# A fused attention, recurrence and MLP step: decode rows second in the output projection, and an up projection that begins before the last token tile is normalised

## What is computed

```
def merge_and_mlp(x, o_a, o_b, mg, w_br_a, w_br_b, w_out, ln1_g, ln1_b, w_up, w_down, ln2_g, ln2_b):
    br_a = jnp.einsum('bse,ed->bsd', o_a, w_br_a)
    br_b = jnp.einsum('bse,ed->bsd', o_b, w_br_b)
    merged = jax.nn.sigmoid(mg[..., :D_MODEL]) * br_a + jax.nn.sigmoid(mg[..., D_MODEL:]) * br_b
    mix = jnp.einsum('bsd,de->bse', merged, w_out)
    x1 = layer_norm(DEEPNORM_ALPHA * x + mix, ln1_g, ln1_b)
    h = jnp.einsum('bsf,fd->bsd', jnp.square(jax.nn.relu(jnp.einsum('bsd,df->bsf', x1, w_up))), w_down)
    return layer_norm(DEEPNORM_ALPHA * x1 + h, ln2_g, ln2_b)
```

## Time and profile before

| | us |
|---|---|
| median of three runs | 2279.09 |
| the three runs | 2273.63, 2279.09, 2280.14 |
| the profiled execution, its own time | 2276.24 |
| its span | 2274.4 |
| PE busy in the span | 2127.7 |
| DVE busy | 1084.1 |
| ACT busy | 744.9 |

### The profile page before, as it was taken

The page is one execution under the profiler, slowest core; times in us unless marked ns, Lnnn a source line. Parts: engine busy times, 40 slices in busy tenths (PEclk is TensorE's granted clock), DMA queues, the critical chain, the costliest instruction groups (busy, mean ns, idle before and its releaser), DMA issues.

```text
span 2274.4 us, 33288 instructions
## 1 busy us (share of the span) xinstructions
PE 2127.7 (94%) x13962; PEld 1804.7 (79%) x13962; DVE 1084.1 (48%) x2075; ACT 744.9 (33%) x1375; POOL 144.4 (6%) x157
## 2 busy tenths in 40 slices
PE   7999899979878999999999999979999999999994
PEld 6997677759548999998888874469888988898883
DVE  2037887746522566765211115544444444444447
ACT  3125666634321355544111112222112221122117
POOL 0021000001110122311000000000000000000003
PEclk9998999989999999999999999979999999999997
DMA  9222000046652232222212131111111111111001
GB/s 235 78 71 106 11 11 1 11 169 213 196 186 66 47 67 53 59 52 85 84 28 56 29 106 61 32 62 47 47 38 56 47 47 37 56 47 47 19 19 75
DMA packets 140193, 156.77 MB, mean 69 GB/s; under 512 B 25794, under 2 KB 122139, under 8 KB 135308
## 3 DMA queue, kind: packets, MB, share of 16 engines
q1 hardware_dynamic: 132012, 111.87, 16.2%
q0 software_dynamic: 8032, 42.78, 6.1%
HBM read 139.05 MB, written 19.76 MB: 70 GB/s over the span
## 4 chain that ended last, share of the span: by engine, by line
PE 85%; DVE 6%; DMA 4%; ACT 3%; issue 2%; SPq 0%; POOLq 0%; POOL 0%; DVEq 0%; ACTq 0%
PE PS L751 57%; PE PS L1294 5%; PE PS L1320 5%; PE PS L951 3%; PE PS L1018 2%; PE PS L932 2%; DMA arena<-in_cache_sel_kv,arena 2%; DVE arena L1794 1%; PE PS L904 1%; PE PS L1003 1%; DVE arena L1810 1%; PE PS L906 1%; DMA arena<-in_x_prompt 1%; PE PS L1220 1%; PE PS L1351 1%
## 5 line engine op out<-in xcount | busy, mean ns | idle before, releaser
L751 PE MATMUL PS<-x_low,w_high_mlp 128*128 128x344 f32 x1104 | 354.1, 321 | 0.0
L751 PE MATMUL PS<-w_down_high,hidden 128*128 128x512 f32 x1024 | 329.5, 397 | 9.9 <-DVE arena L2280 5.6
L751 PE MATMUL PS<-x_high,w_high_mlp 128*128 128x344 f32 x768 | 246.2, 321 | 5.2 <-DVE w_low L772 5.2
L751 PEld LDWEIGHTS PS<-w_down_high,hidden 128*128 128x128 f32 x1024 | 193.3, 189 | 67.9 <-DVE arena L2280 20.2
L751 PE MATMUL PS<-x_high,w_low 128*128 128x344 f32 x768 | 246.7, 321 | 0.0
L2280 DVE TENSOR_TENSOR arena<-arena,PS 128x512 f32<-128x512 f32 x256 | 175.2, 687 | 143.1 <-PE PS L751 143.1
L751 PEld LDWEIGHTS PS<-x_low,w_high_mlp 128*128 128x128 f32 x1104 | 208.1, 188 | 2.6
L751 PE MATMUL PS<-w_down_low,hidden 128*128 128x512 f32 x512 | 201.8, 394 | 0.0
L751 PE MATMUL PS<-x_low,w_high_hgrn 128*128 128x344 f32 x624 | 201.0, 322 | 0.0
L751 PE MATMUL PS<-x_high_a,w_low 128*128 128x344 f32 x480 | 154.7, 322 | 0.0
L751 PE MATMUL PS<-x_high_b,w_low 128*128 128x344 f32 x480 | 153.4, 320 | 0.0
(11 more groups left out here) (347 smaller groups left out, 4025.2 us busy)
## 6 DMA issues: line engine op xcount, KB each, us to landing
wring<-in_w_in SPq DMA_DIRECT2D x100, 256.0 KB, 3.4
wring<-in_w_up SPq DMA_DIRECT2D x64, 256.0 KB, 3.3
arena<-in_w_down SPq DMA_DIRECT2D x16, 1024.0 KB, 4.9
arena<-in_x_prompt SPq DMA_DIRECT2D x16, 512.0 KB, 5.5
x_high_kept<-x_high_att SPq DMA_DIRECT2D x1, 4128.0 KB, 13.6
arena<-in_cache_win_kv SPq DMA_DIRECT2D x8, 512.0 KB, 5.3
arena<-in_w_out SPq DMA_DIRECT2D x2, 2048.0 KB, 9.3
out<-arena SPq DMA_DIRECT2D x8, 512.0 KB
```

The costliest lines, as they stand in the source:

```text
L751: mm = pe.matmul(out, w, x, start=(start and k == 0 and i == 0), stop=(stop and k == tiles - 1 and i == 2))
```

## The change

1. **Order of the tiles.** A list `LN_ORDER` puts the decode rows second: 0, 8, 1, 2, ..., 7. All of the stage's buffers and semaphore counts go by the position p in that list, no longer by the tile number. SP's loads of the residual rows follow the same order. The decode mix now goes to the banks of its position (2 and 3), and DVE's count of finished residuals includes it.
2. **First two weight blocks.** Their high parts get a place of their own, `whU`, in a part of the arena that is free during the output projection. ACT splits them after the copies of position 4, DVE after the work of position 5. The blocks from the third on use `whM` as before.
3. **Order of the first six chunks.** `UP_ORDER` interleaves the first two blocks: chunk 0 of block 0, chunk 1 of block 0, chunks 0 and 1 of block 1, then chunk 2 of both. On PE, chunk (0, 0) stands right behind the transpose of position 7, and the transpose of position 8 (tile 7) stands between the third and the fourth chunk. The waits of each chunk name the tiles it reads. Banks of the chunks are turned by two. ACT has three relus between the reciprocal root of position 8 and its copies. The square of block 0 waits for five relus in place of three.
4. **Second norm's gain and bias.** DVE waits for `ln2_in` where it first uses them, in `shift`, and no longer ahead of the MLP.

```diff
+        whU = rounded("w_high_up", arena_at, 2 * D, 2, KD, P)
+        LN_ORDER = [0, NQ, *range(1, NQ)]
+        UP_ORDER = [(0, 0), (0, 1), (1, 0), (1, 1), (0, 2), (1, 2)]
+        UP_ORDER += [(i, ci) for i in range(2, F_FF // P) for ci in range(3)]
+        def up_high(i):
+            return whU[:, i] if i < 2 else whM[:, i % 2]
+        def up_chunks(i):
+            return (5, 6)[i] if i < 2 else 3 * (i + 1)
...
-            return u_ps, 3 * (n + 1 - (U_U - U_M))
+            return u_ps, 3 * U_M + up_chunks(n - U_U)
...
@@ tensor @@
-            for t in range(NQ + 1):
-                if t >= 2:
-                    pe.wait_ge(f_dve, t - 1)
+            for p, t in enumerate(LN_ORDER):
+                if p >= 2:
+                    pe.wait_ge(f_dve, p - 1)
...
-                if t >= 1:
-                    turn_x1(t - 1)
+                if p >= 1:
+                    turn_x1(p - 1)
+            def up(y):
+                i, ci = UP_ORDER[y]
+                c0, cn = CHUNKS[ci]
+                if ci == 0:
+                    pe.wait_ge(wl_dve, SPLITS_U + i + 1)
+                if y >= 4:
+                    pe.wait_ge(relu_act, y - 3)
+                split_product(pe, PS[:, (y + 2) % 4, 0:cn], [up_high(i)[:, k] for k in range(KD)],
+                              [wl[:, (U_U + i) % WR, k] for k in range(KD)], [x1h[:, k, c0:c0 + cn] for k in range(KD)],
+                              [xl[:, k, c0:c0 + cn] for k in range(KD)]).then_inc(u_ps, 1)
+            pe.wait_ge(x1l_dve, 2 * 4)
+            pe.wait_ge(f_dve, NQ)
+            up(0)
+            pe.wait_ge(x1l_dve, 2 * 7)
+            up(1)
+            pe.wait_ge(f_dve, NQ + 1)
+            up(2)
             turn_x1(NQ)
+            up(3)
             pe.wait_ge(x1l_dve, 2 * (NQ + 1))
+            up(4)
+            up(5)
...
@@ scalar @@
+                rstd_of(p)
+                if p == NQ:
+                    for y in range(3):
+                        relu(y)
                 for half in range(2):
...
-            act.wait_ge(f_ps, NQ + 1)
-            for i in range(2):
-                split_high(act, U_U + i, whM[:, i])
+                if p == 4:
+                    for i in range(2):
+                        split_high(act, U_U + i, up_high(i))
...
@@ vector @@
+                if p == 5:
+                    for i in range(2):
+                        split_low(dve, U_U + i, SPLITS_U + i, up_high(i))
+            x1_low(NQ)
+            x1_scaled(NQ)
+            dve.wait_ge(x1_sc, NQ + 1)
...
-            dve.wait_ge(ln2_in, 32)
-            for i in range(2):
-                split_low(dve, U_U + i, SPLITS_U + i, whM[:, i])
...
-                dve.wait_ge(relu_act, 3 * (i + 1))
+                dve.wait_ge(relu_act, up_chunks(i))
...
             def shift(t):
+                dve.wait_ge(ln2_in, 32)
                 dve.wait_ge(l2_g, t + 1)
```

More of the change, by code:

```diff
@@ L1371, in _ @@
             for g in range(NG):
-                up(2 * g)
-                up(2 * g + 1)
                 if g == 0:
                     down_decode(0)
+                else:
+                    for y in range(6 * g, 6 * g + 6):
+                        up(y)
                 if g >= 1:
@@ L1658, in _ @@
                     act.wait_ge(dn_ps, 16 * (g - 1))
-                for ci, (c0, cn) in enumerate(CHUNKS):
-                    act.wait_ge(u_ps, 3 * (U_U + i - (U_U - U_M)) + ci + 1)
-                    act.activation(uT[g % 2][:, i % 2, 0, c0:c0 + cn], PS[:, (3 * i + ci) % 4, 0:cn], ACT.Relu).then_inc(relu_act, 1)
+                for y in range(max(3, up_chunks(i - 1)) if i else 3, up_chunks(i)):
+                    relu(y)
                 act.wait_ge(sq_dve, i + 1)
@@ L2169, in _, with norm @@
             lc = Steps(dve, ln_c)
-            def norm(t, done):
+            def norm(p, done):
+                t = LN_ORDER[p]
                 n = toks(t)
@@ L2181, in norm, with x1_low @@
                 dve.tensor_tensor(y, y, lng[0:n, 1, :], ALU.add).then_inc(done, 1)
+            def x1_low(p):
+                t = LN_ORDER[p]
+                for half in range(2):
+                    dve.wait_ge(xt1_act, 2 * p + half + 1)
+                    at = (slice(None), slice(4 * half, 4 * half + 4), slice(P * t, P * t + toks(t)))
+                    dve.tensor_tensor(xl[at], PS[:, 4 + 2 * (p % 2) + half, :].rearrange("p (j n) -> p j n", j=4)[:, :, 0:toks(t)],
+                                      x1h[at].bitcast(F32), ALU.subtract).then_inc(x1l_dve, 1)
@@ new lines, in x1_scaled @@
+            def x1_scaled(p):
+                y = x1[0:toks(LN_ORDER[p]), LN_ORDER[p], :]
+                dve.wait_ge(x1_s, p + 1)
+                dve.tensor_scalar(y, y, ALPHA, None, ALU.mult).then_inc(x1_sc, 1)
+            dve.wait_ge(ln_in, 32)
+            for p, t in enumerate(LN_ORDER):
+                dve.wait_ge(f_ps, p + 1)
+                dve.wait_ge(xr_in[p % 2], 16 * (p // 2 + 1))
+                if t < NQ:
+                    dve.scalar_tensor_tensor(out=x1[:, t, :], in0=xr[:, p % 2, :], scalar=ALPHA,
+                                             in1=PS[:, 2 * (p % 2):2 * (p % 2) + 2, :].rearrange("p a n -> p (a n)"),
+                                             op0=ALU.mult, op1=ALU.add).then_inc(f_dve, 1)
+                else:
+                    for half in range(2):
+                        lc(dve.scalar_tensor_tensor(out=x1[0:NB, NQ, 512 * half:512 * (half + 1)],
+                                                    in0=xr[0:NB, p % 2, 512 * half:512 * (half + 1)], scalar=ALPHA,
+                                                    in1=PS[32 * half:32 * half + NB, 2 * (p % 2), :], op0=ALU.mult, op1=ALU.add))
+                    for half in range(2):
+                        y = x1[0:NB, NQ, 512 * half:512 * (half + 1)]
+                        ins = dve.tensor_tensor(y, y, PS[64 + 32 * half:64 + 32 * half + NB, 2 * (p % 2), :], ALU.add)
+                    ins.then_inc(f_dve, 1)
+                dve.wait_ge(f_dve, p + 1)
+                norm(p, x1_s)
+                if p >= 1:
+                    x1_low(p - 1)
+                    x1_scaled(p - 1)
+                if p == 5:
+                    for i in range(2):
+                        split_low(dve, U_U + i, SPLITS_U + i, up_high(i))
@@ L2187, in add_decode @@
                     lc(dve.tensor_tensor(y, y, PS[64 + 32 * half:64 + 32 * half + NB, bank, :], ALU.add))
[L2189 to L2217, removed]
```

64 lines of the change are left out of this document (28 added, 36 removed).

## The result

| | before | after |
|---|---|---|
| median of six runs, us | 2277.63 | 2263.54 |
| lowest and highest | 2273.63, 2280.14 | 2256.92, 2268.55 |
| profiled execution, its own time | 2276.24 | 2268.55 |
| its span | 2274.4 | 2266.7 |

The ratio of the runs is 0.9942, with a 95% interval of 0.9924 to 0.9959. The change makes the kernel faster by 9 to 17 us, 0.4 to 0.8%. The forecast was 2263.1.

What follows compares the result with a forecast made beforehand. PE was busy 2127.7 of 2274.4 us, so only its waits and lower-clock time could be won. Tail -25.7 plus head +11.5 gave -14.2 us; from 2277.3 that is 2263.1 us, range 2257.5 to 2270.

Steps and rivals of the forecast that it cites:

- the stretch: PE from the start of mix 0 to the start of the first down_decode; forecast sum -25.7 + 11.5 = -14.2 us.
- The tail: PE from the end of mix 7 to the first down_decode: 27.5 us instead of 53.2, 25.7 less.
- The covers: PE's work after mix 7 hides tile 7's norm with 3.9 us to spare and its low part with 2.
- The weight splits: ACT and DVE around positions 4 and 5: 4.4 us against 4.7 of idle time, cost taken as 0.
- The growth at down_decode: PE's wait for the second square ahead of the first down_decode: 2.8 us, 0.9 more than before.
- The head: PE's time up to the end of mix 7: 8.4 + 2.6 + 0.5 = 11.5 us added.
- The gap: PE between the decode mix and the turn of tile 0: waits 4.8 us for tile 0's norm.
- The lower clock: PE's clock falls while it idles before tile 0's turn; cost 1.6 to 3.5 us, taken as 2.6.
- The turn of the decode rows: PE's transpose of the decode rows between later mixes: 0.5 us at the upper clock, its wait covered.
- The base: Whole-kernel time the saving is taken from: 2277.3 us, the mean of all four executions.
- The rival at down_decode: PE's clock also falls in the idle time at the first down_decode, costing 1.6 to 3.5 us: 2265.7; chance 0.28.
- The slower rivals: Clock stays low after tile 0's turn: through both next mixes 2288.3 us, chance 0.03; only mix 1 2274.4, chance 0.04.

Runs made afterwards that it cites:

- the third block first: Kernel after, with the third weight block split before the first square on ACT and DVE: 153.5 us from mix 0 to first down_decode; one run 2267.44 us.
- the head's gap removed: Kernel after, with tile 0's turn back behind mix 1 and ACT's decode-row root ahead of its tile 0 copies: 2257.36 us, ratio to before 0.9911.
- the order alone: Kernel before plus only the new tile order (decode rows second): 169.0 us from mix 0 to first down_decode; one run 2283.99 us.
- the splits alone: Kernel before plus only the first two weight blocks split early into `whU`: 163.7 us from mix 0 to first down_decode; one run 2279.10 us.
- the head kept busy: Kernel after plus five unused float32 matmuls in PE's 4.7 us head gap: 152.0 us from mix 0 to first down_decode; one run 2259.78 us.
- the order undone: Kernel after with decode rows last again, four chunks before their turn: 147.9 us from mix 0 to first down_decode; one run 2255.86 us.

## Why the prediction was right

Time and sum came out together: 14.2 us less were forecast and 14.2 measured in the stretch, and 14.1 lie between the medians. The stretch is the evidence. The interval of the ratio leaves 9 to 17 us, so that 2263.1 against 2263.54 is closer than the runs can tell, and in part luck.

- **The tail** was forecast at 27.5 us instead of 53.2 and is 27.5. The covers held with the margins given: 3.9 us for the turn of tile 7, two for its low part. The weight splits fitted into positions 4 and 5 without a wait. The growth at down_decode was forecast as 0.9 and is 0.9 (2.89 against 1.97; the prediction's 2.8 for the wait should be 2.9 by its own 27.5 less 24.6), and the run with the third block first shows its cause.
- **The head** was forecast at 11.5 us more and is 11.5: mix 0 to the turn of tile 6 takes 1489.22 - 1362.45 = 126.8 us, before 1470.21 - 1354.98 = 115.2. The gap is 4.74 where 4.8 stood in the sum. The lower clock was sized at 2.6 and cost 2.2 (4.6 us at the lower level, not 5.2); it lay in the range of 1.6 to 3.5 taken from three resumptions. The turn of the decode rows, estimated at 0.5, takes 0.66 at the upper clock (in the run with the head's gap removed). That the sum still meets 11.5 is luck of a few tenths: the 0.4 too much for the clock was made up by the decode rows' turn and by the mixes beside the narrow work, which stood in no term (mix 0 takes 13.93 us to the start of the decode mix; before, the first two mixes took 27.57, or 13.79 each).
- **The base** was the mean of the four times then known, 2277.3; the median of six is 2277.63. Taking the profiled execution alone as the base would have given 2262.0, the median of three 2264.9; all three lie within the spread of after's runs, so that the choice of base was not tested.
- **The rival at down_decode** did not happen in the profile of after: PEclk stayed 1.00 behind its gap of 2.9 us. But it does happen, in two of the eight profiles with such a gap, as the last section shows. It then cost 1.6 us, the low end of the range given.
- **The slower rivals** had no trace: the clock came back after 4.6 us.

What the forecast did not ask is whether the order was needed. It took the head's 11.5 us as the price of the tail's gain. The runs show that 6.4 of it (154.3 against 147.9) buys nothing: with the decode rows last, two thirds of both blocks (four chunks, 15 us) cover both norms.

## What to carry to other kernels

An edit that moves a short item behind the first long one uncovers the chain that the second long one had hidden; look at both ends of the loop and not only at the one being mended. When work is found that can fill a wait, ask again whether the reordering that was meant to remove the wait is still needed. Measure such a change by a stretch of the trace that both kernels share, since it shows tenths of a microsecond where whole runs of one kernel differ by half a per cent.

## What the runs showed of the hardware

**The clock after like gaps is not always the same.** The gap ahead of the first down_decode, followed each time by 1.04 us of narrow matmuls, is 1.97 or 1.98 us in four profiles: the kernel before, the order alone, the splits alone, and the third block first. Behind it the clock held in three of them; before, PEclk was 1.00. With the splits alone it fell, one microsecond after PE had resumed at 1525.54:

```profile
1526.00:1528.00 2.00, 2.00 (x13) 1.49 (x6) 1.56 (x2) 2.00 (x3) 0.00 (x0) 0.64 0.99 256
1528.00:1530.00 2.00, 2.00 (x8) 2.00 (x8) 1.62 (x2) 1.15 (x1) 0.00 (x0) 0.50 0.74 266
```

The gap is 2.89 us in the other four: the kernel after, the head kept busy, the head's gap removed, and the order undone. The clock held in three again, the kernel after among them, and fell in the one with the head kept busy (the first row is of after, the second of that one):

```profile
1516.00:1520.00 4.00, 3.27 (x22) 2.44 (x23) 2.94 (x4) 3.46 (x3) 0.00 (x0) 1.00 0.81 264
```

```profile
1508.00:1510.00 2.00, 2.00 (x8) 2.00 (x8) 1.61 (x3) 1.84 (x2) 0.00 (x0) 0.50 0.70 268
```

Both falls show in the time from the first down_decode to the last matmul of the last one: 675.6 us in each, against 674.1 in the six others. In these eight profiles such a gap thus cost either itself or itself and 1.6 more, and its length did not tell which. What decides it was not tried.

**Most of the spread between the profiled executions arises ahead of the change.** In the ten profiled executions mix 0 starts at 1354.1, 1354.2, 1355.0, 1355.1, 1358.1, 1361.8, 1361.9, 1362.1, 1362.5 and 1362.5 us, though everything ahead of it is the same. Between the profiles of before and after, 4.3 of the 7.5 us come up between 179 and 470 us, in the prompt's attention. One spell at the lower clock stands there that the kernel before has not; 420 to 440 us of before, then of after:

```profile
420.00:440.00 20.00, 18.92 (x183) 14.57 (x181) 14.98 (x41) 14.27 (x45) 0.00 (x0) 1.00 0.00 1
```

```profile
420.00:440.00 20.00, 18.24 (x141) 13.39 (x141) 13.98 (x39) 13.81 (x46) 0.00 (x0) 0.83 0.00 1
```

The spells go with the starts: added up from the granted clock's records in the traces, PE's clock is at the lower level for 71.7 to 75.1 us ahead of mix 0 in the four profiles that start it by 1355.1, for 85.3 in the one that starts it at 1358.1, and for 92.1 to 95.6 in the five that start it from 1361.8 on. That the spells are the cause, and the whole of it, is not shown: no run changed them.
